# VectorE's order in the RWKV-7 groups of a hybrid decoder layer drawn up anew, and one decay product moved to GpSimd

## The reference, cut to what matters

```python
w = -jax.nn.softplus(-(w0 + jnp.tanh(w_lo) @ w_w2)) - 0.5
decay = jnp.exp(-jnp.exp(w.astype(jnp.float32)))
a = jax.nn.sigmoid(a0 + a_lo @ w_a2)
kk = (k * k_k).reshape(B, S, H, N).astype(jnp.float32)
kk = kk / jnp.maximum(jnp.sqrt(jnp.sum(kk * kk, axis=-1, keepdims=True)), 1e-12)
k = k * (1.0 + (a - 1.0) * k_a)
...
    sa = jnp.einsum('bhvk,bhk->bhv', state, -kk_t)
    state = (state * w_t[:, :, None, :]
             + sa[..., None] * (kk_t * a_t)[:, :, None, :]
             + v_t[..., None] * k_t[:, :, None, :])
    return state, jnp.einsum('bhvk,bhk->bhv', state, r_t)
...
o = (o - mu) * lax.rsqrt(var + GN_EPS)
```

## Time and profile before

| | us |
|---|---|
| median of 3 runs (2066.12 to 2069.53) | 2067.25 |
| the profiled execution | 2067.76 |
| its span, first to last instruction | 2066.0 |
| TensorE busy | 2026.0 |
| VectorE busy | 1155.8 |
| ScalarE busy | 861.7 |
| GpSimd busy | 142.6 |

### The profile page before, as it was taken

The page is one execution under the profiler, slowest core; times in us unless marked ns, Lnnn a source line. Parts: engine busy times, 40 slices in busy tenths (PEclk is TensorE's granted clock), DMA queues, the critical chain, the costliest instruction groups (busy, mean ns, idle before and its releaser), DMA issues.

```text
span 2066.0 us, 27601 instructions
## 1 busy us (share of the span) xinstructions
PE 2026.0 (98%) x11416; PEld 1691.7 (82%) x11416; DVE 1155.8 (56%) x1023; ACT 861.7 (42%) x833; POOL 142.6 (7%) x113
## 2 busy tenths in 40 slices
PE   8999999999999999999897999999999999999999
PEld 6888888888888889888776888888888888888887
DVE  4455545555455565766788545455554555545564
ACT  6333333343343355854333345433333433333353
POOL 0000000000000000344323100000000000000000
PEclk9999999999999999999999999999999999999999
DMA  7565555555555547666312455656555655556554
GB/s 260 185 200 185 186 196 186 193 188 188 192 193 186 189 150 221 205 195 209 99 41 69 148 190 183 196 184 195 191 184 192 192 188 188 193 187 199 184 184 143
DMA packets 190049, 373.62 MB, mean 181 GB/s; under 512 B 7110, under 2 KB 16962, under 8 KB 189980
## 3 DMA queue, kind: packets, MB, share of 16 engines
q1 hardware_dynamic: 186300, 361.47, 54.2%
q0 software_dynamic: 3680, 11.15, 1.9%
HBM read 363.94 MB, written 5.52 MB: 179 GB/s over the span
## 4 chain that ended last, share of the span: by engine, by line
PE 92%; DVE 5%; issue 1%; POOL 0%; DMA 0%; ACT 0%; SPq 0%; DVEq 0%; POOLq 0%
PE PS L363 29%; PE PS L364 29%; PE PS L365 29%; PE PS L420 1%; PE PS L384 1%; DVE X L1653 0%; DVE XT L1666 0%; PE PS L1334 0%; DMA x_resid<-in_x 0%; DVE kk L1577 0%; DVE wlo L349 0%; PE PS L1298 0%; DVE AB L1639 0%; DVE AK L1639 0%; DVE k L1593 0%
## 5 line engine op out<-in xcount | busy, mean ns | idle before, releaser
L349 DVE TENSOR_TENSOR wlo<-raw,whi 128x2048 fp32r<-128x2048 f32 (+1 forms) x338 | 777.5, 2300 | 762.5 <-PE PS L365 757.3
L340 ACT ACTIVATE whi<-raw 128x2048 fp32r<-128x2048 f32 (+1 forms) x338 | 643.2, 1904 | 988.7 <-PE PS L365 980.4
L363 PE MATMUL PS<-whi,xT_hi 128*128 128x512 f32 (+2 forms) x1936 | 752.5, 389 | 0.0
L365 PE MATMUL PS<-whi,xT_lo 128*128 128x512 f32 (+2 forms) x1936 | 747.9, 386 | 0.0
L364 PE MATMUL PS<-wlo,xT_hi 128*128 128x512 f32 (+2 forms) x1936 | 747.5, 386 | 0.0
L365 PEld LDWEIGHTS PS<-whi,xT_lo 128*128 128x128 f32 x1936 | 363.5, 188 | 73.4
L363 PEld LDWEIGHTS PS<-whi,xT_hi 128*128 128x128 f32 x1936 | 363.6, 188 | 72.2 <-issue 0.4
L364 PEld LDWEIGHTS PS<-wlo,xT_hi 128*128 128x128 f32 x1936 | 363.7, 188 | 71.6
L363 PE MATMUL PS<-whi,hT_hi 128*128 128x512 f32 x680 | 264.8, 389 | 0.1
L365 PE MATMUL PS<-whi,hT_lo 128*128 128x512 f32 x680 | 264.6, 389 | 0.0
L364 PE MATMUL PS<-wlo,hT_hi 128*128 128x512 f32 x680 | 264.5, 389 | 0.0
(11 more groups left out here) (330 smaller groups left out, 1112.1 us busy)
## 6 DMA issues: line engine op xcount, KB each, us to landing
raw<-in_w_gate SPq DMA_DIRECT2D x88, 1024.0 KB, 5.2
raw<-in_w_up SPq DMA_DIRECT2D x88, 1024.0 KB, 5.2
raw<-in_w_down SPq DMA_DIRECT2D x88, 1024.0 KB, 5.1
...
```

Of the source, the lines that this page charges most:

```text
L340: nc.scalar.activation(whi[:, n % WHI, 0:wd], raw[:, n % RAW, 0:wd], ACT.Copy).then_inc(hi_ready, 1)
L349: nc.vector.tensor_tensor(wlo[:, n % WLO, 0:wd], raw[:, n % RAW, 0:wd], f32(whi[:, n % WHI, 0:wd]), ALU.subtract).then_inc(lo_ready, 1)
L363: nc.tensor.matmul(acc, a, whi[:, n % WHI, c], start=st, stop=False)
L365: ins = nc.tensor.matmul(acc, b, whi[:, n % WHI, c], start=False, stop=en)
```

## The change

The exclusive running sum of the decay (the constant `cum_ex`, four products on TensorE for each group) goes. ScalarE forms from `sigw` the exponential that undoes a token's own decay, and `pex` is then that times `pin`: on VectorE for group 0, on GpSimd (`decay_ahead`) for groups 1 to 3. The gate products have four parts, so none stands at level 3 in groups 1 and 2. The two squares (of the key, and of the centred result, the last group's excepted) and the copy of `W1T` go from VectorE to ScalarE. VectorE's steps change places: `out_centre` before level 0, `out_spread` and the bonus between levels 0 and 1, the rest of `front` by the new table. `pe_out` moves ahead of `pe_state`, to another bank of PSUM, and `out_lo` ahead of the first state update. GpSimd forms `pex` of group r + 2 inside `finish(r)`, and `key_norm` comes last. The last group's `finish` ends with three operations on VectorE (`out_last`). In group 3 the splits of the first two blocks of the output projection move one level later on VectorE.

```diff
-        "cum_ex": rate / 2 * (same & (s < t)),
         "cum_all": rate / 2 * ((s // CHUNK) == np.arange(2)[None, :]),
         "from_in": rate / 2 * (cs + 1.0),
         "half_from_inv": -rate / 2 * (cs + 1.0) - np.log(2.0),
-        "from_ex": rate / 2 * cs,
+        "own_undone": np.full((P, 1), -rate / 2),
...
+        def decay_ahead(pool, r):
+
+            pool.wait_ge(exps_ready, 5 * r + 3)
+            nc.gpsimd.tensor_tensor(fr(r).pex[:, :, :], fr(r).pex[:, :, :], fr(r).pin[:, :, :], ALU.mult).then_inc(undone, 1)
...
+                if r < GROUPS - 2:
+                    decay_ahead(pool, r + 2)
                 pool.wait_ge(out_var, r + 1)
                 power(hsg[:, 1, :], "minus_half", out_pow)
-                if r < GROUPS - 2:
-                    key_norm(pool, r + 2)
+                if r == GROUPS - 1:
+                    return
                 pool.wait_ge(out_pow, r + 1)
...
+            decay_ahead(pool, 1)
             key_norm(pool, 1)
+            gate_ahead(0)
             for r in range(GROUPS):
-                gate_ahead(r)
                 finish(r)
+                if r < GROUPS - 1:
+                    gate_ahead(r + 1)
+                if r < GROUPS - 2:
+                    key_norm(pool, r + 2)
...
-                    pe.wait_ge(gates_ready, 2 * r + 2)
-                    ins = nc.tensor.matmul(two, const("cum_ex"), mine[:, t, :], start=True, stop=True)
...
+                if it:
+                    pe_out(pe, it - 1)
...
+                nc.scalar.activation(fr(r).pex[:, :, :], fr(r).sigw[:, :, :], ACT.Exp, bias=const("own_undone"),
+                                     scale=HALF_RATE).then_inc(exps_ready, 1)
...
+        def act_square_key(act, r):
+            act.wait_ge(kk_scaled, r + 1)
+            nc.scalar.activation(tmp[:, :, :], fr(r).kk[:, :, :], ACT.Square).then_inc(kk_squared, 1)
+
+        def act_square_out(act, r):
+            act.wait_ge(out_centred, r + 1)
+            nc.scalar.activation(tmp[:, :, :], oo[:, :, :], ACT.Square).then_inc(out_squared, 1)
...
-                if r == GROUPS - 1 and n in LATER[:2]:
+                if r == GROUPS - 1 and n == 2:
                     act.wait_ge(front_ready, 4 * GROUPS)
-                    split_hi(act, WOUT + n - LATER[0])
+                    split_hi(act, WOUT)
+                if r == GROUPS - 1 and n == 4:
+                    act.wait_ge(bonus_ready, GROUPS)
+                    split_hi(act, WOUT + 1)
...
+            if r:
+                act_out(act, r - 1)
+            act.wait_ge(w1_done, r + 1)
+            nc.scalar.activation(W1T[:, :, :, :].rearrange("p a t (c n) -> p c (a t) n", c=2),
+                                 PS[:, 4:6, 0:256].rearrange("p c (x n) -> p c x n", x=4), ACT.Copy).then_inc(w1_ready, 1)
...
-                    tt(kk[:, :, :], k_, bc_t(gc[:, 0, :]), ALU.mult)
-                    tt(tmn[:, :, :], kk[:, :, :], kk[:, :, :], ALU.mult)
-                    v.reduce_sum(hsf[:, 0, :], by_head(tmn[:, :, :]), axis=X_AXIS).then_inc(kk_var, 1)
-                elif step == "own key":
-                    dve.wait_ge(kk_var, r + 1)
+                    v.tensor_tensor(kk[:, :, :], k_, bc_t(gc[:, 0, :]), ALU.mult).then_inc(kk_scaled, 1)
+                elif step == "key sum":
+
+                    if r == 0:
+                        dve.wait_ge(kk_scaled, 1)
+                        tt(tmn[:, :, :], kk[:, :, :], kk[:, :, :], ALU.mult)
+                    else:
+                        dve.wait_ge(kk_squared, r)
+                    v.reduce_sum(hsf[:, 0, :], by_head(tmp[:, :, :] if r else tmn[:, :, :]), axis=X_AXIS).then_inc(kk_var, 1)
+                elif step == "key share":
+                    if r == 0:
+                        dve.wait_ge(kk_var, 1)
                     dve.wait_ge(gates_ready, 2 * r + 2)
                     chain(v.scalar_tensor_tensor(tmn[:, :, :], aa[:, :, :], -1.0, bc_t(gc[:, 1, :]), ALU.add, ALU.mult))
+                elif step == "own key":
...
-                            for step in {2: ("key",), 3: ("own key", "read"), 4: ("unit key", "learned")}[n]:
+                            for step in {2: ("key", "key share"), 3: ("key sum", "own key"), 4: ("unit key", "learned")}[n]:
                                 front(nxt, step)
-                        elif n in LATER[:2] and h == 1:
+                        elif n in LATER[1:] and h == 1:
                             dve.wait_ge(front_ready, 4 * GROUPS)
-                            split_lo(dve, WOUT + n - LATER[0])
+                            split_lo(dve, WOUT + n - LATER[1])
                         if heads and h == 1:
                             dve_heads_lo(dve, n)
                         if before is not None and (n, h) == (0, 1):
-                            out_centre(before)
-                        if before is not None and (n, h) == (1, 1):
                             out_spread(before)
+                            front(r, "bonus")
             def state(r, nxt):
-                dve.wait_ge(w1_done, r + 1)
-                v.tensor_copy(W1T[:, :, :, :].rearrange("p a t (c n) -> p c (a t) n", c=2),
-                              PS[:, 4:6, 0:256].rearrange("p c (x n) -> p c x n", x=4)).then_inc(w1_ready, 1)
-                if nxt is not None:
-                    front(nxt, "read gain")
+                if r:
+                    out_lo(r - 1)
...
-                    if c == 1 and r:
-                        out_lo(r - 1)
-                    if nxt is not None and c == 0:
-                        front(nxt, "read sum")
                     if nxt is not None:
                         if c == 0:
                             dve.wait_ge(exps_ready, 5 * nxt + 5)
+                            dve.wait_ge(undone, nxt)
+                        if c == 1:
+                            front(nxt, "read")
                         for k in ((0,), (1,), (2, 3), ())[c]:
                             with_decay(nxt, k)
+                        if c == 3:
+                            front(nxt, "read gain")
...
+            def out_last(r):
+
+                dve.wait_ge(norm_used, r + 1)
+                dve.wait_ge(out_pow, r + 1)
+                tt(by_head(og[:, :, :]), by_head(og[:, :, :]), per_head(hsg[:, 1, :]), ALU.mult)
+                tt(og[:, :, :], og[:, :, :], bonus[:, r % 2, :, :], ALU.add)
+                dve.wait_ge(exps_ready, 5 * r + 5)
+                v.tensor_tensor(og[:, :, :], og[:, :, :], out_gate(r), ALU.mult).then_inc(o_ready, 1)
...
-                    front(nxt, "bonus")
+                    front(nxt, "read sum")
                     keys_out(nxt)
                 add_inner(it, 1)
                 if nxt is not None:
                     scores(nxt)
+                    out_centre(it)
                     inverse(nxt, EARLY, None, it)
             out_centre(GROUPS - 1)
             out_spread(GROUPS - 1)
+            out_last(GROUPS - 1)
```

52 lines of the change are left out of this document (31 added, 21 removed).

## The result

The changed kernel takes 2054.59 us (median of four runs, 2052.78 to 2055.31) against 2067.94 for the kernel before on the same chip: a ratio of 0.9934 with a 95% interval from 0.9917 to 0.9952. The profiled execution took 2054.1 us, its span 2052.2, which is 13.8 less than before. Measured again on another chip, on which the kernel before had 2066.9, the changed kernel took 2057.03: a gain of 9.9 us where the first measurement has 13.4 (ratio 0.9951, 0.9938 to 0.9965). So the gain is some 10 to 13 us, and a median is not to be read to a tenth of a microsecond.

The account below looks back on a forecast made before the run. VectorE's queue order and length set the RWKV-7 stage's pace, with TensorE close behind. Savings of 4.1 + 2.4 + 1.3 + 3.7 + 0.8 = 12.3 us gave a 2055.0 us median, range 2049 to 2060.5.

Parts of the forecast that it names:

- Group 1, 4.1 forecast: RWKV-7 stage, group 1: VectorE's new order saves 4.1 us, one blocked step charged at 1.3; bounds 2.0 and 6.0.
- the read steps that were to cost nothing: Group 1, behind the first update of `U`: the read steps moved there fill waits and cost nothing.
- the second rival: More is saved: blocked steps miss GpSimd and TensorE keeps its 2.4 GHz level; about 17.5 us, 2049.8; chance 0.14.
- Group 2, 2.4 forecast: Same order as group 1, so 34.9 us against 37.36: 2.4 saved; bounds 0.5 and 4.8.
- Group 0, 1.3 forecast: Group 0 loses 0.2 to 0.7 at `alpha`, gains square, W1T's copy and an own-key step: 1.3 net; bounds 0 and 2.6.
- Group 3 and the end, 4.5 forecast: Group 3 saves 3.7 us (bounds 2 and 5), the last steps at the end 0.8 (bounds 0.3 and 1.0).
- the second split's move: Group 3: the second `wlo`, blocked by GpSimd ahead of level 4, moves behind it, saving 3.0 us.
- The transposes and the last steps: Group 3: `og` transposes no longer stand behind `S`, 0.7 us; at the end VectorE steps replace three on GpSimd, 0.8.
- The removed product at level 3 is worth nothing: TensorE, level 3: removing the product part gains nothing as VectorE is late there; otherwise up to 1 us.
- The power holds VectorE too: Rival: GpSimd's power keeps VectorE out for 1.63 us in three groups; 7.4 us saved, 2059.9; chance 0.16.
- slower: Rival: five VectorE steps per group wait for GpSimd and the power comes late; 9 us slower, 2076; chance 0.03.
- Nothing shortened: Rival: ScalarE's added work delays copies TensorE needs and TensorE's products become the bound; about 2065; chance 0.05.

Follow-up runs that it names:

- the order alone: The changed kernel with the old decay products back (four on TensorE, gate products in five parts): 2051.65 us, ratio 0.9919.
- the two bonus kernels: GpSimd's bonus step moved to the next group's start: on the changed kernel 2055.27 us; on old decay products with changed order and late own key 2053.17 us.

## Why the prediction was right, point by point

The median came out at 2054.59 against 2055.0. That this is 0.4 is luck, twice over. Groups 1 and 2 gave 2.5 us more than their terms and group 3 with the end 2.5 less, and these cancelled; of the 1.5 that the profiled span gained beyond the sum, 0.9 came with the first loads and 0.6 with group 0. And the second measurement, on another chip, has a gain of 9.9 us where the sum has 12.3. What was right is the mechanism: VectorE's order set the pace, and the order alone gives the whole gain of groups 1 and 2.

**Group 1, 4.1 forecast, 5.33 measured.** The steps held. The first two levels kept their starts; one blocked step was charged and there is one; the power was to end 1 us behind and VectorE waits 0.99; the own key is at 0.68. Level 4 was through 19.92 us into the group (20.45 forecast) and `S` at 23.41 (24.15). Up to the first `U` 3.89 were gained where the sum had 3.1, in part because the blocked step cost 1.07 instead of 1.3. Behind it 1.44 were gained where the sum had 1.0, but not by the step that the sum named. It took the whole difference between group 1's 3.89 and group 0's 2.90 for `xT_lo`. Group 2 of the kernel before, with the same code at a clock of 1.00, took 3.18, so the early `xT_lo` was worth 0.48, and 0.71 of the interval was group 1's low clock (0.73 there). And the read steps that were to cost nothing cost 0.73 at the end of the group. Without the clock the stretch behind the first `U` would have lost 0.23; the clock's 1.67, which I had put into the second rival, covers it. Undone alone, the squares cost the most, 2.06 up to `S`, and I had not valued them by themselves.

**Group 2, 2.4 forecast, 3.66 measured.** The reason, that it takes the same time as group 1, was right to a hundredth (33.70 both), and so was the reading that it had been the faster one for its clock: 39.03 less 37.36 is the 1.67 above. The number carried group 1's error over: 3.89 up to the first `U`, 0.48 and 0.02 between the updates, less 0.73 at the tail.

**Group 0, 1.3 forecast, 1.88 measured** in the one trace. It can't be told closer: in kernels whose order there is all but the same it took between 34.8 and 36.3 us, and once 39.64, where GpSimd's mixing came first. The start was to lose 0.2 to 0.7. The product for `pex` takes over the blocked turn whole (2.86, and `alpha` then 0.69), as said. Leaving out the 0.9 from the first loads, the start came 0.06 earlier, which no run here separates from nothing: the first `AB` of the changed kernel stands at 993.36 in one profile and at 996.32 in the other.

**Group 3 and the end, 4.5 forecast, 1.96 measured.** This is the mis-sized term. Up to `S` 3.11 were gained, but the second split's move is worth only 2.02 there, where I had 3.0. In the new order, with the splits back, the second one is no longer blocked by GpSimd (2.29 instead of 3.14) and waits 1.04 instead of 1.20, so there was less to save. The rest of the order, which I had not counted in this group, gives 1.54, and the stop ahead of `S` takes 0.45. The transposes and the last steps were to give 1.5 behind `S`; with no stop they give 1.53 (19.29 to 17.76), without a wait for GpSimd. The changed kernel loses 2.68 there again to TensorE's stop of 1.90 and the low clock after it. No row of the kernel before showed such a stop of 0.45 or more in the stage, and no rival of mine had it. Put together from the two stretches without a stop (20.84 up to `S` and 17.55 behind it) group 3 would take about 38.4 us, an estimate: 5.3 less than before, so without the stops the 4.5 would have been too little.

**The removed product at level 3 is worth nothing** was right, and its condition fits: up to 1 us once VectorE isn't late, about 0.9 by the comparison of the two bonus kernels. **The power holds VectorE too** is wrong in the direction I feared and right in the other. `k` and the bonus took 0.68 beside it; it is the power that grows, from 1.63 to 1.96 and 2.02. The rival *slower* says that it decides from about 5.5 us lost in a group; by its own terms the changed kernel is even with the old one at 4.3 + 4.5 / 3 = 5.8. **Nothing shortened** and **slower** found no support in groups 1 and 2: ScalarE's added work did not hold TensorE, whose longer waits there (0.4 us and more) are all for VectorE, and VectorE lost one turn in each of them, not five.
